# Zero-padded new values, z's last tile through ScalarE's queue, and a later sigmoid in one step of a hybrid decoder

## What is computed

```python
proj = rmsnorm(x) @ w_in                       # q, k, v, indexer, u, gates ga and gb
attn = sparse_attention(q, k_all, v_all, ...)  # k_all = cached pages + the new keys
y_a  = attn @ w_attn_proj
z    = gelu(s5_scan(u))
glu_a, glu_g = split(z @ w_glu)
y_b  = glu_a * sigmoid(glu_g)
x    = x + (sigmoid(ga) * y_a + sigmoid(gb) * y_b) @ w_out
x    = x + conv_ffn(rmsnorm(x))
```

## Time and profile before

| | before |
|---|---|
| median of three runs | 1541.27 us (1540.31 to 1541.33) |
| the profiled execution: own time / span | 1541.73 us / 1539.9 us |
| granted TensorE clock over the span | 0.998 |
| TensorE (PE) busy | 1527.9 us, 99% |
| VectorE (DVE) busy | 1023.2 us, 66% |
| ScalarE (ACT) busy | 666.5 us, 43% |
| GpSimd (POOL) busy | 460.9 us, 30% |
| DMA, mean over the span | 183 GB/s |

### The profile page before, as it was taken

How to read it: one execution, slowest core, us unless ns; L and a number is a source line. 1 busy time by engine, 2 the same in 40 slices (tenths; PEclk the granted TensorE clock), 3 DMA queues, 4 the chain that set the end, 5 groups by cost and what they waited for, 6 DMA issues and landing times.

```text
span 1539.9 us, 33758 instructions
## 1 busy us (share of the span) xinstructions
PE 1527.9 (99%) x12448; PEld 1511.5 (98%) x12448; DVE 1023.2 (66%) x1477; ACT 666.5 (43%) x901; POOL 460.9 (30%) x581
## 2 busy tenths in 40 slices
PE   8999999999999999999999999999999999999998
PEld 8999999999999999999999999999999999999998
DVE  7655788888666676657676767677777764444443
ACT  6344355544666644444333333333333333333332
POOL 8992478877422201221111111111111100001100
PEclk9999999999999999999999999999999999999999
DMA  8886577676766586565555555454545475555552
GB/s 260 240 208 180 144 211 217 194 214 191 242 216 192 159 203 214 163 212 178 164 166 161 169 158 174 153 177 150 178 149 182 147 226 175 173 174 175 168 179 91
DMA packets 300222, 282.16 MB, mean 183 GB/s; under 512 B 35280, under 2 KB 292832, under 8 KB 300000
## 3 DMA queue, kind: packets, MB, share of 16 engines
q1 hardware_dynamic: 283968, 256.70, 55.3%
q10 hardware_dynamic: 13840, 16.62, 3.5%
q0 software_dynamic: 2320, 7.54, 1.5%
HBM read 266.73 MB, written 14.05 MB: 182 GB/s over the span
## 4 chain that ended last, share of the span: by engine, by line
PE 87%; DVE 0%; issue 0%; DVEq 0%; ACT 0%; ACTq 0%
PE banks L579 28%; PE banks L581 28%; PE banks L580 28%; PE banks L589 0%; PE banks L774 0%; PE banks L815 0%; PE banks L724 0%; PE banks L787 0%; PE banks L711 0%; PE banks L828 0%; PE banks L733 0%; PE banks L636 0%; DVE yo L1866 0%; PE banks L830 0%; DVE wlo L1325 0%; PE banks L900 0%
## 5 line engine op out<-in xcount | busy, mean ns | idle before, releaser
L1325 DVE TENSOR_TENSOR wlo<-raw,whi 128x1024 fp32r<-128x1024 f32 x443 | 558.6, 1273 | 288.0 <-ACT whi L953 283.6
L953 ACT ACTIVATE whi<-raw 128x1024 fp32r<-128x1024 f32 x443 | 462.4, 1051 | 547.4 <-PE banks L581 498.7
L580 PE MATMUL banks<-h_lo,whi 128*128 128x288 f32 x1408 | 415.7, 295 | 0.0
L581 PE MATMUL banks<-h_hi,wlo 128*128 128x288 f32 x1408 | 415.7, 295 | 0.0
L579 PE MATMUL banks<-h_hi,whi 128*128 128x288 f32 x1408 | 414.6, 294 | 0.0
L579 PE MATMUL banks<-hhi,whi 128*128 128x288 f32 (+1 forms) x912 | 271.8, 298 | 3.4 <-DVE hlo L1351 3.1
L581 PE MATMUL banks<-hhi,wlo 128*128 128x288 f32 (+1 forms) x912 | 269.8, 296 | 0.0
L580 PE MATMUL banks<-hlo,whi 128*128 128x288 f32 (+1 forms) x912 | 269.7, 296 | 0.0
L580 PEld LDWEIGHTS banks<-h_lo,whi 128*128 128x128 f32 x1408 | 264.6, 188 | 0.1
L581 PEld LDWEIGHTS banks<-h_hi,wlo 128*128 128x128 f32 x1408 | 264.4, 188 | 0.0
L579 PEld LDWEIGHTS banks<-h_hi,whi 128*128 128x128 f32 x1408 | 264.1, 188 | 0.1
(11 more groups left out here) (354 smaller groups left out, 2160.2 us busy)
## 6 DMA issues: line engine op xcount, KB each, us to landing
raw<-in_w_up SPq DMA_DIRECT2D x352, 256.0 KB, 3.4
raw<-in_w_in SPq DMA_DIRECT2D x223, 256.0 KB, 3.4
raw<-in_w_down SPq DMA_DIRECT2D x176, 256.0 KB, 3.0
raw<-in_w_glu SPq DMA_DIRECT2D x64, 256.0 KB, 3.5
raw<-in_w_out SPq DMA_DIRECT2D x64, 256.0 KB, 3.2
raw<-in_w_attn_proj SPq DMA_DIRECT2D x32, 256.0 KB, 3.9
scratch_gates<-gt ACTq DMA_DIRECT2D x16, 288.0 KB, 4.2
gbt<-scratch_gates POOLq DMA_DIRECT2D x8, 288.0 KB, 3.7
```

The source lines that it names most:

```text
L580: pe.matmul(out, h, xl[:, kt, :], start=False, stop=False)
L581: mm = pe.matmul(out, lo, xh[:, kt, :], start=False, stop=kt == nk - 1)
L953: act.activation(whi[:, s, :, 0:cols], raw[:, s, :, 0:cols], ACT.Copy).then_inc(hi_ready, 1)
L1325: dve.tensor_tensor(wlo[:, s, :, 0:cols], raw[:, s, :, 0:cols], whi[:, s, :, 0:cols], ALU.subtract).then_inc(lo_ready, 1)
```

## The change

1. `vnew`, the samples' new values, becomes a tile of 128 rows of which the last 124 are zero, and so do the rows of the third part of `pTb`. The matmuls of line 830 then run over 128 rows like those of line 828, with the same products. POOL clears the two `vnew` buffers in the last gate turn and `pTb[:, 2, :]` after its last `turn_forward`; SP and ScalarE wait for that before they first write there.
2. ScalarE issues the four stores of z's last tile right after its `gelu(7)`, and the four loads after `hi(C_GLU, 0)`. POOL issues them no more.
3. ScalarE's `store_gates(0, ...)` for the last gates moves behind the sigmoid of GLU unit 0's gate half. POOL waits for that store only before `gate_branch(7)`, which reads those gates.
4. VectorE does `z_low(6)` ahead of the last `gate_evac`, not behind it.
5. The stores of the two states share one semaphore, so ScalarE ends with one wait fewer.

```diff
-    vnew = [at(f"vnew{i}", [DS, KV], F32, GR + 8192 + 1024 * i) for i in range(2)]
+    vnew = [at(f"vnew{i}", [P, KV], F32, GR + 8192 + 1024 * i) for i in range(2)]
...
                 if j:
                     sp.wait_ge(sem("sv_ready"), j)
+                else:
+                    sp.wait_ge(sem("new_cleared"), 2)
...
-                            if g < NPAGES:
-                                mm = pe.matmul(o, pTb[:, g, k], vpg[b][:, g, c], start=g == 0, stop=False)
-                            else:
-                                mm = pe.matmul(o, pTb[0:DS, 2, k], vnew[b][:, c], start=False, stop=True)
+                            values = vpg[b][:, g, c] if g < NPAGES else vnew[b][:, c]
+                            mm = pe.matmul(o, pTb[:, g, k], values, start=g == 0, stop=g == NPAGES)
...
                 hi(c, 6)
                 if not more:
                     gelu(it)
+                    z_out(act, it)
                 hi(c, 7)
                 store_gates(1, 7 + it, 4 * it)
...
             hi(C_GLU, 0)
+            z_in(act, NUT - 1)
             hi(C_GLU, 1)
             z_high(NUT - 2)
-            store_gates(0, 7 + N_GATE, 4 * N_GATE - 2)
             act.activation(spare[:, 0:1], ident[:, 0:1], ACT.Exp)
...
                 act.wait_ge(sem("spt_t"), j + 1)
+                if j == 0:
+                    act.wait_ge(sem("new_cleared"), 3)
...
+                if i == 0:
+                    store_gates(0, 7 + N_GATE, 4 * N_GATE - 2)
                 hi(c, 5)
...
-            act.wait_ge(sem("s5_stored"), 16)
-            act.wait_ge(sem("conv_stored"), 16)
+            act.wait_ge(sem("states_stored"), 16 * 2)
...
             lo(C_GLU, 1)
+            z_low(NUT - 2)
             gate_evac(0, 6 + N_GATE, C_GLU)
-            z_low(NUT - 2)
...
                     stage_values(0)
+                    for b in range(2):
+                        pool.memset(vnew[b][:, :], 0.0).then_inc(sem("new_cleared"), 1)
...
+            pool.memset(pTb[:, 2, :], 0.0).then_inc(sem("new_cleared"), 1)
             new_keys(1)
-            z_out(pool, NUT - 1)
...
-            z_in(pool, NUT - 1)
...
-            for par in range(2):
-                pool.wait_ge(sem(f"gates_out{par}"), 16 * N_GATE)
+            pool.wait_ge(sem("gates_out0"), 16 * N_GATE - 16)
+            pool.wait_ge(sem("gates_out1"), 16 * N_GATE)
...
+                if i == N_GLU - 1:
+                    pool.wait_ge(sem("gates_out0"), 16 * N_GATE)
```

More of the change, by code:

```diff
@@ L488, in values_in @@
                     sp.wait_ge(sem("sv_ready"), j)
+                else:
+                    sp.wait_ge(sem("new_cleared"), 2)
                 for b in range(2):
                     i = 2 * j + b
-                    sp.dma_start(vnew[b][:, :], W["v_new"][DS * i:DS * (i + 1), :]).then_inc(sem("v_in"), 16)
+                    sp.dma_start(vnew[b][0:DS, :], W["v_new"][DS * i:DS * (i + 1), :]).then_inc(sem("v_in"), 16)
                     for g, page in enumerate(pages(i)):
@@ L2110, in _ @@
                 turn_forward(it)
+            pool.memset(pTb[:, 2, :], 0.0).then_inc(sem("new_cleared"), 1)
             new_keys(1)
-            z_out(pool, NUT - 1)
             pool.wait_ge(sem("masks_ready"), 1)
             pool.dma_start(W["mask"], wk[2][:, :]).then_inc(sem("mask_out"), 16)
-            z_in(pool, NUT - 1)
             pool.wait_ge(sem("last_ready"), 2 * N_GATE)
-            pool.dma_start(O["s5_state"], last[:, :, :, :].rearrange("p c k i -> p (c k i)")).then_inc(sem("s5_stored"), 16)
+            pool.dma_start(O["s5_state"], last[:, :, :, :].rearrange("p c k i -> p (c k i)")).then_inc(sem("states_stored"), 16)
             for par in range(2):
@@ L2188, in _ @@
             pool.wait_ge(sem("cst_saved"), 2 * N_UP + 1)
-            pool.dma_start(O["conv_state"], cstate[:, :, :].rearrange("p a b -> p (a b)")).then_inc(sem("conv_stored"), 16)
+            pool.dma_start(O["conv_state"], cstate[:, :, :].rearrange("p a b -> p (a b)")).then_inc(sem("states_stored"), 16)
             for k in range(7):
```

## The result

| | before | changed |
|---|---|---|
| median of 19 runs each | 1540.15 us (1539.50 to 1541.70) | 1543.21 us (1541.64 to 1545.04) |
| ratio, 95% interval | | 1.0019, 1.0013 to 1.0026 |
| the profiled execution: own time / span | 1541.73 / 1539.9 us | 1542.92 / 1541.1 us |
| granted TensorE clock over the span | 0.998 | 0.998 |

The kernel has become 3.1 us slower. The busy times of the page tell nothing of it: TensorE does 1.1 us less than before in a longer span.

The account below looks back on a forecast made before the run. TensorE, busy 1527.9 of 1539.9 us, was taken to bound the kernel. The terms -0.48 + 0.13 + 0.05 = -0.3 us, against a median of 1541.27, gave 1541.0 us, no change, range 1540.0 to 1542.6.

Parts of the forecast that it names:

- Part 1: Line 830's blocks of 8 in four calls: 128 rows take 0.06 us off each, 0.48 us off TensorE's work.
- the drain rival: Line 830's blocks on TensorE: a change of shape is dear, full tiles win up to 1.9 us, 1539.6; chance 2%.
- Part 2: ScalarE issuing z's last tile: the last gate chunk's rounding and `hi(C_GLU, 1)` each come 2.5 us later.
- Part 3: VectorE between the stages: later `z_low(7)` gives TensorE a new 0.4 us wait; unit 0 as a whole +0.13 us.
- the old wait at unit 0's middle: TensorE's wait for `p_ready` ahead of unit 0's middle, 0.27 us, claimed to go.
- the slower rival: Unit 0's second chunk: late-landing stores make ScalarE's loads and `z_low(7)` 3.3 us late, 1544.3; 15% with milder form, 4% beyond 0.2%.
- Part 4: The sigmoid behind unit 0 delays `p_ready` and `o_rows_ready` for unit 1: +0.05 us, between 0 and +0.5.
- part 5: One wait fewer at the kernel's end, after the last stores: 0.04 us at most, taken as 0.
- milder form: Before unit 0's second chunk, POOL beside both `z_low`, or a store landing of 5 us: 1541.8 to 1542.6; within the 15%.

Follow-up runs that it names:

- the bridge: The changed kernel with 24 more matmuls, whose result nobody reads, ahead of TensorE's wait for z's last tile: 1542.09 us, ratio 1.0014 against before.

## Why the prediction was wrong

**Part 1, mis-sized.** I priced line 830's block of 8 at its neighbour's 22.5 ns a record and so took 0.06 us from each of eight blocks, 0.48 in all with 0.96 as the bound. It is 1.56. The step that failed is "with 128 rows I let the eight records cost what their neighbours do": the neighbour's 0.36 us had a change of shape in it as well, so its 22.5 ns a record, which I took for the norm, are 14 ns and a share of that change. Two equations in two unknowns were on the page (the earlier trace rows has blocks of 16 and of 8): if a record costs the same in both, (0.36 - 0.24) / 8 = 15 ns, and 0.12 us are left for each block. I gave the drain rival 2% and a gain of 1.9 us; in kind it was right.

**Part 2, the issues and what stands behind them: half right.** Eight issues came where I put them and delayed the last gate chunk by 3.1 us instead of 2.5 (I had all four stores at 0.58, the first took 1.11), without cost, as the kernel with the stores alone shows. "The last store lands 2.6 to 4.6 us later" is the step that failed: 6.27. Those figures came from the four stores of one execution, issued by POOL, and I let them bound four stores under another load. One thing that differs is POOL's next large store: it had stood behind a wait, and the change takes that wait away; I followed the removed waits of POOL to its staging and not to the store in between. Whether it lengthens the landing is open, but holding it back gained 3.0 us. The delay of `hi(C_GLU, 1)` is so 5.4 us instead of 2.5: 0.6 more from the stores' issues, 2.1 from the landing (397.61 + 1.6 - 396.5, less those 0.6), 0.1 from the loads'.

**Part 3, the mechanism right and its size off.** The list on VectorE, its order and its durations came out within 0.2 us (from the start of `lo` to the end of `z_low(7)` 406.13 - 401.39 = 4.74 us, forecast 1.2 + 0.37 + 0.68 + 2.2 + 0.46 = 4.9), and the old wait at unit 0's middle went as said. The wait became 2.85 instead of 0.4 us, from what part 2 had wrong, the landing above all. The two `z_low` that I bounded at 0.99 took 0.46 (in two of the other profiles the first of them took 0.92). The old wait of 0.27 us was one execution's: in the kernel with one change of shape fewer, whose unit 0 is before's, the stretch from head to head takes 413.91 - 398.07 = 15.84 us instead of 16.09 and TensorE doesn't wait.

**A term that was missing.** Nothing was put down for TensorE's clock. That the wait would be hidden but for 0.4 us left no reason to look there, and the slower rival, which had a wait of over 3 us, needed the term too. A wait of 2.7 us was followed by 3.4 at the lower level, 1.5 us on top: a third of the loss that unit 0 has.

**Part 4, right.** The later sigmoid cost 0.14 us in the profile (forecast 0.05, between 0 and 0.5), and nothing that the runs of the kernel with the last tile on POOL can tell. POOL's clearings and **part 5** came out as nought.

**The slower rival** was what happened, in place and in mechanism: stores that land late, ScalarE idle at its first load, `z_low(7)` late by about 3 us, 1544.3. That its 3.0 us above before are nearly the measured 3.1 is luck: its landing of 7.5 us was 1.2 too long and its full tiles won 1.1 too little, and it had nothing for the clock's 1.5. I gave it 15% with its milder form and 4% beyond 0.2%. The chance was too low because I weighed only how often one landing would be long. What decided was how the margin was built: in before, 3.8 us of POOL's waiting for this landing lay beside other work; the change put the same wait in front of the rounding on which VectorE, and through it TensorE, depends, where `z_low(7)` had 0.34 us to spare. And the rule cited in part 2 (the Trainium skill, "DMA: Bandwidth & Descriptors", Issuing engines are not separate DMA queues) spoke against this step and got no weight in the chances; the traces agree with it in so far as nothing was won in landing by ScalarE's issuing: its stores had landed 4.4 to 6.7 us after the last issue in seven profiles, POOL's within 3.5 to 4.9 us of their issue in five.

## What to carry to other kernels

A wait for a DMA is priced by what stands behind it on the engine that waits, and its landing time not by the few landings of one old execution; the loads here cost nothing two instructions further down. When a change takes a wait off an engine, list everything that this wait held back, transfers above all, for it comes forward too. A wait of TensorE should be priced with the clock behind it. And short matmuls of another shape between long ones should be counted by their changes of shape.

## What was not expected of the hardware

- A change between 128 and 4 rows of contraction costs TensorE 0.13 us each time, on 14 ns a record of 64 columns; the rows themselves cost nothing.
- One wait of 2.7 us in a stream of matmuls was followed by 3.4 us at 1.2 GHz. Waits of 1.5 us (without full tiles), 1.6 (the state's store kept behind), and 0.6 with 1.9 behind it (`z_low(7)` first) were followed by none; in the windows from 400 to 415 us the changed kernel alone is below 1.00, at 0.89. Near the start, waits of 2.1 and 2.3 us were followed by such a stretch (the bridge, before) and ten of 0.4 to 1.7 us were not; this moves two traces by 1.6 us against each other.
- Four stores of 36 KB had landed between 3.5 and 6.7 us after the last issue began, in eight profiles of the same place in the program; each of the four took 2.6 to 4.6 us in before.
- The first DMA that ScalarE issues behind `gelu(7)` took it 1.1 to 1.3 us in each of seven profiles, the next ones 0.5 to 0.7.
